# Dilated mixer: the rotary swap of the eight later tiles moves from TensorE to ScalarE

## The reference, cut to what matters

```python
proj = xn @ w_in_dil[slot]
q, k, v, qm = jnp.split(proj, [D_MIX, 2 * D_MIX, 3 * D_MIX], axis=-1)
qh = apply_rope(split_heads(q, N_MIX_HEADS), cos, sin)
kh = apply_rope(split_heads(k, N_MIX_HEADS), cos, sin)
mix = dilated_attention(qh, kh, split_heads(v, N_MIX_HEADS))

def apply_rope(x, cos, sin):
    x1, x2 = jnp.split(x.astype(jnp.float32), 2, axis=-1)
    y = jnp.concatenate([x1 * cos - x2 * sin, x2 * cos + x1 * sin], axis=-1)
```

## Time and profile before

| | |
|---|---|
| median of 3 runs | 1814.13 us |
| the profiled execution | 1817.73 us |
| its span, first to last instruction | 1815.9 us |
| mean granted TensorE clock | 0.994 |
| TensorE busy (matmul) | 1768.4 us, 97% |
| VectorE busy | 939.3 us, 52% |
| ScalarE busy | 517.1 us, 28% |
| GpSimd busy | 1014.1 us, 56% |
| swap matmuls (two recorded for each swap) | 24, of 590 to 697 ns |

### The profile page before, as it was taken

How to read it: one execution, slowest core, us unless ns; L and a number is a source line. 1 busy time by engine, 2 the same in 40 slices (tenths; PEclk the granted TensorE clock), 3 DMA queues, 4 the chain that set the end, 5 groups by cost and what they waited for, 6 DMA issues and landing times.

```text
span 1815.9 us, 24424 instructions
## 1 busy us (share of the span) xinstructions
PE 1768.4 (97%) x9583; PEld 1405.5 (77%) x9588; DVE 939.3 (52%) x1896; ACT 517.1 (28%) x1151; POOL 1014.1 (56%) x1046
## 2 busy tenths in 40 slices
PE   7999999999899999999999999999999999999998
PEld 6886678676668877779888888896667888888886
DVE  5976644694543355424662166236665356415642
ACT  3614533312532344423110011033444211101111
POOL 7623366553337733345776777555333577677762
PEclk9999999999999999999999999999999999999999
DMA  5220323221223312113323332322111233333331
GB/s 176 82 77 21 114 77 99 71 81 56 73 76 105 112 51 71 47 47 98 107 87 111 93 93 88 110 70 79 62 47 47 64 99 105 102 96 93 94 102 48
DMA packets 170994, 151.16 MB, mean 83 GB/s; under 512 B 5192, under 2 KB 145992, under 8 KB 170880
## 3 DMA queue, kind: packets, MB, share of 16 engines
q1 hardware_dynamic: 169280, 148.12, 26.5%
q10 hardware_dynamic: 1600, 1.48, 0.3%
HBM read 147.45 MB, written 2.14 MB: 82 GB/s over the span
## 4 chain that ended last, share of the span: by engine, by line
PE 93%; DVE 4%; ACT 2%; issue 1%; another core or an unknown queue 0%; DMA 0%; ACTq 0%; DVEq 0%
PE ps L281 77%; PE ps L1987 3%; PE ps L2020 2%; PE ps L2005 2%; PE ps L352 1%; PE ps L640 1%; PE ps L1486 1%; PE ps L1993 1%; PE ps L1963 1%; PE ps L1464 1%; PE ps L1407 1%; PE ps L1415 1%; PE ps L665 1%; PE ps L1423 0%; PE ps L672 0%
## 5 line engine op out<-in xcount | busy, mean ns | idle before, releaser
L127 POOL TENSOR_SCALAR w_hi<-w_raw 128x512 fp32r<-128x512 f32 x520 | 314.6, 631 | 758.7 <-PE ps L281 754.1
L131 POOL TENSOR_TENSOR w_lo<-w_raw,w_hi 128x512 fp32r<-128x512 f32 x520 | 694.6, 1366 | 11.3
L281 PE MATMUL ps<-x_hi,w_hi 128*128 128x512 f32 (+1 forms) x1448 | 537.9, 371 | 0.7 <-DVE x_lo L434 0.7
L281 PE MATMUL ps<-x_hi,w_lo 128*128 128x512 f32 (+1 forms) x1448 | 527.8, 364 | 0.0
L281 PE MATMUL ps<-x_lo,w_hi 128*128 128x512 f32 (+1 forms) x1448 | 527.4, 364 | 0.0
L281 PEld LDWEIGHTS ps<-x_hi,w_hi 128*128 128x128 f32 x1448 | 274.7, 190 | 69.3 <-issue 20.0
L281 PEld LDWEIGHTS ps<-x_hi,w_lo 128*128 128x128 f32 x1448 | 274.3, 189 | 44.0
L281 PEld LDWEIGHTS ps<-x_lo,w_hi 128*128 128x128 f32 x1448 | 274.8, 190 | 40.6 <-issue 0.5
L2281 DVE SCALAR_TENSOR_TENSOR ffn_cv<-ps,col,ffn_cv 128x510 f32<-128x510 f32 (+1 forms) x176 | 131.8, 749 | 192.5 <-ACT ffn_cv L2259 187.8
L2259 ACT ACTIVATE ffn_cv<-ps,col 128x512 f32<-128x512 f32 x88 | 63.7, 776 | 500.2 <-PE ps L281 500.2
L309 DVE TENSOR_TENSOR h<-h,ps 128x512 f32<-128x512 f32 x64 | 43.9, 688 | 261.5 <-PE ps L281 261.4
(11 more groups left out here) (345 smaller groups left out, 2425.2 us busy)
## 6 DMA issues: line engine op xcount, KB each, us to landing
w_raw<-w_up SPq DMA_DIRECT2D x88, 512.0 KB, 5.0
w_raw<-w_down SPq DMA_DIRECT2D x16, 1024.0 KB, 5.0
w_raw<-od_w_in SPq DMA_DIRECT2D x12, 1024.0 KB, 5.2
w_raw<-w_in_fox SPq DMA_DIRECT2D x10, 1024.0 KB, 5.4
w_raw<-w_in_dil SPq DMA_DIRECT2D x10, 1024.0 KB, 5.0
w_raw<-w_out SPq DMA_DIRECT2D x8, 1024.0 KB, 5.1
w_raw<-ev_w_in SPq DMA_DIRECT2D x7, 1024.0 KB, 5.5
w_raw<-w_down SPq DMA_DIRECT2D x8, 768.0 KB, 4.4
```

Of the source, the lines that this page charges most:

```text
L127: ins = pool.tensor_scalar(hi[:, c:min(c + PIECE, size)], raw[:, c:min(c + PIECE, size)], 1.0, 1.0, ALU.mult, ALU.mult)
L131: ins = pool.tensor_tensor(lo[:, c:min(c + PIECE, size)], raw[:, c:min(c + PIECE, size)], hi[:, c:min(c + PIECE, size)].bitcast(F32), ALU. ...
L281: mm = pe.matmul(o, l, r, start=start and i == 0, stop=stop and i == 2)
```

## The change

ScalarE makes the swap of tiles 4 to 11 from the projection in PSUM, just ahead of the tile's evacuation and in the same place of its queue: four copies of 32 rows by 512, each from the group of rows beside its own, with scale -1 or 1, into bank 5. TensorE's swaps of these tiles go; those of tiles 0 to 3 stay. ScalarE waits for `swap_free` first, as TensorE did. VectorE's `rope` of these tiles waits for the four copies (`act_swapped`) and for the tile's evacuation, since it works in place on the evacuated tile.

```diff
+                self.turned_by_act[m] = len(self.rope_tiles)
                 self.rope_tiles.append((dst, 2 * i + j, m))
...
                 for s in range(self.N):
-                    if s in self.swaps:
-                        swap(self.swaps[s])
                     if s + 1 < self.N:
                         scores(s + 1)
...
+                        if m in self.turned_by_act:
+                            act.wait_ge(self.swap_free, self.turned_by_act[m])
+                            for q in range(4):
+                                ins = act.activation(ps[32 * q:32 * q + 32, 5, :], ps[32 * (q ^ 1):32 * (q ^ 1) + 32, bank, :], ACT.Copy,
+                                                     scale=1.0 if q % 2 else -1.0)
+                            ins.then_inc(self.act_swapped, 1)
                         act.activation(dst, ps[:, bank, 0:dst.shape[1]], ACT.Copy).then_inc(self.evacuated.s, 1)
...
-                    dve.wait_ge(self.swapped, i + 1)
+                    if i < 4:
+                        dve.wait_ge(self.swapped, i + 1)
+                    else:
+                        dve.wait_ge(self.act_swapped, i - 3)
+                        dve.wait_ge(self.evacuated.s, self.evacuated.at(m + 1))
                     dve.tensor_tensor(tmp, ps[:, 5, :], self.sin[:, :], ALU.mult).then_inc(self.swap_free, 1)
```

More of the change, by code:

```diff
@@ L1840, in __init__ @@
                     self.cos, self.sin, self.swap = at("rope_cos", 74, [P, S]), at("rope_sin", 76, [P, S]), at("rope_swap", 78, [P, P])
-                    self.tables_in, self.swapped, self.swap_free, self.roped = (sem(n) for n in ("rope_in", "swapped", "swap_free", "roped"))
+                    self.tables_in, self.swapped, self.act_swapped, self.swap_free, self.roped = (
+                        sem(n) for n in ("rope_in", "swapped", "act_swapped", "swap_free", "roped"))
                 n = 2 * self.N
@@ L1890, in __init__ @@
                 self.steps = [(i, p, qb) for i, p in enumerate(self.SEQ) for qb in range(T)]
-                self.swaps = {}
+                self.swaps, self.turned_by_act = {}, {}
                 self.rope_tiles = []
@@ L2147, in rope @@
                 def rope(i):
-                    dst, tile, _ = self.rope_tiles[i]
+                    dst, tile, m = self.rope_tiles[i]
                     x, tmp = dst[:, tile, :], self.tmp[:, i % 2, :]
-                    dve.wait_ge(self.swapped, i + 1)
+                    if i < 4:
[3 more added lines that the diff above has]
+                        dve.wait_ge(self.evacuated.s, self.evacuated.at(m + 1))
                     dve.tensor_tensor(tmp, ps[:, 5, :], self.sin[:, :], ALU.mult).then_inc(self.swap_free, 1)
```

## The result

| | before | changed |
|---|---|---|
| median, first measurement | 1818.35 us (6 runs, 1814.03 to 1820.20) | 1807.62 us (6 runs, 1804.42 to 1811.04) |
| median, measured again | 1816.98 us (13 runs) | 1808.93 us (6 runs, 1806.62 to 1814.01) |
| ratio, first measurement | | 0.9941, 95% interval 0.9925 to 0.9957 |
| ratio, measured again | | 0.9948, 95% interval 0.9932 to 0.9965 |
| span of the profiled execution | 1815.9 us | 1805.2 us |

What follows compares the result with a forecast made beforehand. TensorE, busy 97% of the span, was taken as the bound. Five swaps at 1.38 us and three at 0.94 save 9.7, added copies cost nothing on the path: 1814.1 - 9.7 = 1804.4 us, range 1802.5 to 1809.5.

Steps and rivals of the forecast that it cites:

- What bounds the kernel: Whole kernel: TensorE, busy 97% of the span; time taken from its queue comes off the end.
- rival 3: Behind the mixer: time is freed but given back at a later stage with its own pace; 1814 us, chance 0.08.
- The price of a swap: TensorE's queue: 1.38 us saved at five turns of four transposes, 0.94 at three of eight; sum 9.7 us.
- The price of the copies: ScalarE, ahead of each evacuation: four copies take 1.96 us per tile, 15.7 us in all, hidden beside TensorE's work.
- the pitch: ScalarE's four copies: time from one start to the next, taken as 0.49 us, high end 0.78, far end 1.15.
- the forecast's own signs: Changed profile: among others, copies at a pitch of 0.49 and no wait of step 24's scores for rope.
- The cover: Mixer steps: TensorE asks for ScalarE's delayed copies late enough to hide them, with 0.8 to 1.1 us to spare.
- s = 7: Mixer loop step 7: values needs both copied halves; 0.84 us of cover left, gone at a pitch of 0.70.
- s = 11: Mixer loop step 11: values follows a token block; 0.95 us of cover left, gone at a pitch of 0.73.
- The tight place: Rope of k tile 4, step 22, needed by step 24's scores: 0.2 us to spare, 0.23 late at pitch 0.60.
- The total: Whole kernel: median of 1814.1 less 9.7 gives 1804.4 us; forecast's chance 0.63.
- rival 4: Whole kernel: the saving is there, but runs fall 4 to 5 us up, near the slowest; 1809 us, chance 0.07.

Runs made afterwards that it cites:

- e9: Against the kernel before: ScalarE swaps only tiles 4, 6, 7, 8 and 10, TensorE keeps 5, 9 and 11; 1811.25 us, ratio 0.9958.
- e4: Kernel before, with TensorE's own swap placed behind the next step's scores instead of ahead of them; 1817.83 us, ratio to before 0.9998.
- e10: Changed kernel with four copies of 32 rows by 128 columns, only the rows read or only the rows written changing; 1810.02 us, executed once.
- e5: Changed kernel with each of the four copies cut into pieces of 256 columns; 1807.00 us, ratio to before 0.9940.
- e7: Changed kernel with each of the four copies cut into pieces of 64 columns; 1815.56 us, ratio to before 0.9995.
- e6: Changed kernel with each of the four copies cut into pieces of 128 columns; 1808.01 us, ratio to before 0.9949.
- e2: Changed kernel with four copies of 128 rows by 128 columns, the swap itself left out; 1810.43 us, executed once.
- e3: Changed kernel with the four 32-row copies written to SBUF instead of PSUM bank 5; 1805.23 us, executed once.
- e11: The changed kernel once more, unaltered, on the chip of the repeated version without TensorE swaps; 1808.93 us.
- e8: Changed kernel with the prelude's four swaps (tiles 0 and 1 of q and k) also made by ScalarE; 1804.07 us, ratio to before 0.9925.
- e12: Changed kernel with the prelude's four swaps also made by ScalarE, measured again; 1802.97 us, ratio to before 0.9911.

## Why the prediction was right

**What bounds the kernel.** Right. Time taken from TensorE's queue came off the end to 0.1 us, and nothing behind the stretch took it back (416.5 and 416.6 us), so rival 3 didn't happen.

**The price of a swap.** Right, 1.38 and 0.94 forecast against 1.37 and 0.93 in e9. The sum was 9.7, the stretch 9.67. That it agrees to the second digit is partly luck: it leaves out the 0.1 us at scores(24). The measured 1.37 are made of two things, as e4 shows; I had put the split at 0.94 of swap and 0.44 of waiting; e4 makes it 0.84 and 0.53, and the first depends on what stands behind the swap.

**The price of the copies.** The term that failed is the pitch: "I take 0.49, since source, size and function are those of that row". It was 0.575, and 2.32 us for a tile instead of 1.96, 18.1 us of busy ScalarE instead of 15.7. The overlap didn't hang on size and function but on the rows (e10). So two of the forecast's own signs came out otherwise: the pitch wasn't 0.49, and scores(24) did wait for rope, by 0.02. The range given (0.49 to 0.78) held it. It didn't matter, because the pitch had to pass 0.70 before TensorE waited for copy(s), and because at k tile 4 a pitch of 0.575 costs 0.1 us.

The bubble that the Trainium skill ("Advanced Engine Details and Errata", TRN2 Errata) describes between ScalarE's instructions showed more strongly in the swap's copies, 2.29 us for four, than in my estimate of 1.9 to 2.1 from the overhead in the Trainium skill's "Perfetto Trace Analysis" (Optimizing Scalar/DVE Operations). Neighbours with unchanged rows still overlap by about 0.1 us, the swap's own copies by nothing.

**The cover.** Right as a model, off by the pitch in size: 0.44 us left at s = 7 where 0.84 stood. e5 to e7 tested it with a longer T. At s = 7 it gives 5.52 for 5.58 measured, and at s = 11 of e6, 1.22 + 2.98 = 4.20 for 4.21. What it left out (under e5 to e7) cost nothing in the changed kernel, since TensorE waited for no copy(s).

**The tight place.** The text had rope of k tile 4 start with 0.2 to spare and be up to 0.23 late at c = 0.60. It was 0.19 late at 0.575, and scores(24) lost under 0.1 us.

**The total.** The difference was right, 9.7 against 9.67 in the stretch and 10.7 and 8.1 in the medians. The time was 3.2 us too low: 1804.4 rests on a median of three runs, two of them at the fast end. More runs put before at 1817 to 1818, and the changed kernel at 1807.6 to 1808.9, within the range but at its far end, where rival 4 (1809) had put it.

## What to carry to other kernels

Price an instruction of the bound engine from start to start of its neighbours, with and without it: the wait ahead of it belongs to the price, and part of that can be had by reordering alone. Before moving it to an idle engine, write down for each place when the bound engine asks for what is queued behind the new work; the smallest of these margins, not the idle share, says how much the idle engine can take. Here 2.3 us for each of the eight tiles cost 0.1 us in all, 3.0 cost 2, and 3.9 took nearly the whole gain back.

## What the runs showed of the hardware

**Neighbouring ScalarE copies of 32 rows overlap only if their rows stay the same.** Four copies of 32 rows by 128 columns: 0.73 us with the same rows (0.07 of overlap each), 1.00 when the rows read or the rows written change from copy to copy. Copies of 128 rows overlap by 0.1. Four of 32 by 512 with changed rows: 2.29 into PSUM, 2.39 into SBUF.

**A copy into PSUM is slightly shorter than into SBUF:** 0.564 against 0.589 us for 32 rows by 512, 0.582 against 0.597 for 128 rows.

**Behind the same idle gap the clock falls in some executions and not in others.** Ahead of the second scores TensorE stood idle 2.69 us in the profile of before, and its granted clock fell to 0.50. In the changed kernel's first profile (its timeline, and the window):

```profile
1243.64 0.70 PE L1989 MATMUL ps<-mix_k,mix_q 64*128 64x256 f32 x4 [2.70 <-DVE mix_stat L2134]
...
1244.00:1246.00 2.00, 2.00 (x12) 1.42 (x8) 1.93 (x7) 0.29 (x2) 2.00 (x3) 1.00 0.00 0
```

It stood idle 2.70 us, and the granted clock stayed at 1.00, the 2.4 GHz level. The first projection part behind this gap took 3.9 to 4.4 us instead of 2.96 in 8 of the 12 profiles that have the gap (before, e2, e3, e4, e7, e9, e10, e11), and 2.94 to 2.97 in the other four. From 1 to 2 us behind the start of the second scores the granted clock is 0.50 in each of the eight (the 1.2 GHz level) and 1.00 in each of the four. With the slower scores that is up to 1.6 us, a part of the spread of 10 us among executions of one kernel. In e8 and e12 the gap is down to 0.6 us, and neither fell. The windows of e4 and before (under e4) show the granted clock below 1.00 in other stretches too; what makes up the rest of the spread wasn't looked into.
